# Branch stage of a two-block layer: weight splits ahead of the sigmoid, and the recurrence's first tap and convolution moved within the tile loop

## The reference, cut to what matters

```python
r = sigmoid(einsum('bsnc,ncd->bsnd', xb, w_r) + b_r)      # xb: x in 8 blocks of 128 channels
i = sigmoid(einsum('bsnc,ncd->bsnd', xb, w_i) + b_i)
log_a = (-8.0 * r) * softplus(-a_param)
a = exp(log_a)
u = sqrt(-expm1(2.0 * log_a)) * (i * x)                   # x: causal convolution of 4 taps before it
h_t = a_t * h_(t-1) + u_t                                  # associative_scan over the sequence
y_rnn = h * gelu(gelu_branch)
g = sigmoid(gates.reshape(bsz, s_len, 3, D_MODEL) + gate_b)
m = g[:,:,0] * (y_rnn @ w_br_rnn) + g[:,:,1] * (y_diff @ w_br_diff) + g[:,:,2] * (y_fox @ w_br_fox)
x = x + m @ w_out
```

## Time and profile before

| | before |
|---|---|
| median of 3 runs | 3139.36 us (3138.09 to 3141.09) |
| span of the profiled execution | 3138.1 us |
| PE busy | 2972.4 us, 95% of the span |
| DVE busy | 1407.6 us, 45% |
| ACT busy | 1139.3 us, 36% |
| POOL busy | 734.5 us, 23% |
| attended loop in the trace | about 606 to 869 us |
| recurrence loop in the trace | about 869 to 1077 us |

### The profile page before, as it was taken

How to read it: one execution, slowest core, us unless ns; L and a number is a source line. 1 busy time by engine, 2 the same in 40 slices (tenths; PEclk the granted TensorE clock), 3 DMA queues, 4 the chain that set the end, 5 groups by cost and what they waited for, 6 DMA issues and landing times. The chain is left out here.

```text
span 3138.1 us, 38141 instructions
## 1 busy us (share of the span) xinstructions
PE 2972.4 (95%) x14814; PEld 2394.9 (76%) x14814; DVE 1407.6 (45%) x2138; ACT 1139.3 (36%) x1581; POOL 734.5 (23%) x396
## 2 busy tenths in 40 slices
PE   8997999899999999999999999989899999999988
PEld 6675766588877788877888887867777888878776
DVE  4366044311145413334444344456533556565776
ACT  4354145322156612233222222243442455324543
POOL 2100100022221222212114422111223333123452
PEclk9998999899999999999999999999999999899989
DMA  3110210122211222231111111124333111223343
GB/s 137 43 41 13 62 34 24 23 62 61 67 51 45 64 61 79 103 79 40 47 40 47 60 47 47 40 74 84 65 107 101 48 34 28 108 47 94 131 145 111
DMA packets 250124, 203.63 MB, mean 65 GB/s; under 512 B 38452, under 2 KB 219140, under 8 KB 249996
## 3 DMA queue, kind: packets, MB, share of 16 engines
q1 hardware_dynamic: 247820, 200.84, 22.0%
q10 hardware_dynamic: 2176, 1.05, 0.2%
HBM read 174.69 MB, written 27.16 MB: 64 GB/s over the span
## 5 line engine op out<-in xcount | busy, mean ns | idle before, releaser
L144 POOL TENSOR_TENSOR w_low<-w_raw,w_high 128x1024 fp32r<-128x1024 f32 (+1 forms) x180 | 414.4, 2302 | 1739.7 <-ACT w_high L137 1736.6
L137 ACT ACTIVATE w_high<-w_raw 128x1024 fp32r<-128x1024 f32 (+1 forms) x180 | 179.5, 997 | 293.3 <-PE mix_banks L162 162.3
L162 PE MATMUL ffn_banks<-act_high,w_high 128*128 128x512 f32 x704 | 275.1, 391 | 4.0 <-POOLq L111 4.0
L162 PE MATMUL ffn_banks<-act_low,w_high 128*128 128x512 f32 x704 | 274.9, 390 | 0.0
L162 PE MATMUL ffn_banks<-act_high,w_low 128*128 128x512 f32 x704 | 274.7, 390 | 0.0
L162 PE MATMUL mix_banks<-act_high,w_high 128*128 128x512 f32 x640 | 254.5, 398 | 6.6 <-POOL w_low L144 4.3
L162 PE MATMUL mix_banks<-act_low,w_high 128*128 128x512 f32 x640 | 250.4, 391 | 0.0
L162 PE MATMUL mix_banks<-act_high,w_low 128*128 128x512 f32 x640 | 250.1, 391 | 0.0
L1788 PE MATMUL ffn_banks<-v_high,f_high 128*128 128x512 f32 x352 | 143.4, 407 | 18.2 <-DVE x L1970 9.8
L162 PEld LDWEIGHTS ffn_banks<-act_high,w_high 128*128 128x128 f32 x704 | 132.7, 188 | 32.1 <-POOLq L111 4.4
L1970 DVE TENSOR_TENSOR x<-x,ffn_banks 128x512 f32<-128x512 f32 x176 | 117.1, 685 | 83.7 <-PE ffn_banks L1788 83.7
(11 more groups left out here) (641 smaller groups left out, 6945.8 us busy)
## 6 DMA issues: line engine op xcount, KB each, us to landing
w_raw<-in_w_in SPq DMA_DIRECT2D x106, 512.0 KB, 4.1
w_raw<-in_ffn_up SPq DMA_DIRECT2D x44, 512.0 KB, 3.8
w_raw<-in_w_out SPq DMA_DIRECT2D x24, 512.0 KB, 3.7
v_raw<-in_ffn_down SPq DMA_DIRECT2D x11, 1024.0 KB, 5.0
decay<-acum_rows SPq DMA_DIRECT2D x16, 512.0 KB, 3.6
exp_c<-exp_acum_rows SPq DMA_DIRECT2D x16, 512.0 KB, 5.3
x_ring<-in_x SPq DMA_DIRECT2D x8, 512.0 KB, 10.3
m_part<-gate SPq DMA_DIRECT2D x8, 512.0 KB
```

Source lines behind the costliest of these rows:

```text
L137: act.activation(self.high[slot][:, 0:nk, :], self.raw[slot][:, 0:nk, :], ACT.Copy).then_inc(self.s("high", slot), 1)
L144: pool.tensor_tensor(self.low[slot][:, 0:nk, :], self.raw[slot][:, 0:nk, :], self.high[slot][:, 0:nk, :].bitcast(F32), ALU.subtract).then_ ...
L162: last = pe.matmul(out[:, h, :] if not halves else out[h], w[slot][:, k, :], x[:, k, cols], start=(n == 0), stop=(n == 3 * nk - 1))
```

## The change

In the attended loop the split of slot 0's next turn moves ahead of the sigmoid of the half; the split of slot 1 stays behind it. In the recurrence the first tap becomes a step of its own, `tap3(n)`: tile 0's is made ahead of the loop, and tile n+1's right behind the sqrt of tile n, ahead of the high part of y. It waits for the product of VectorE that reads `xc` (`ix`) in place of `xc_free`, which goes away. On VectorE the convolution becomes `conv(n)`: tile 0's ahead of the loop, tile n+1's between y and y's low part of tile n. VectorE's loop becomes an `over_loop` too. The activations and the VectorE operations are the same in kind and number.

```diff
                 def attended_turn(n, more):
                     for j in two:
+                        turn = n * 2 + j + 1
+                        W.split_high(act, 0, turn if more or j == 0 else RNN_AT)
                         sigmoid_attended(n, j)
-                        turn = n * 2 + j + 1
                         if more or j == 0:
-                            W.split_high(act, 0, turn)
                             W.split_high(act, 1, turn, NK)
                         else:
-                            W.split_high(act, 0, RNN_AT)
                             W.split_high(act, 1, RNN_AT)
...
-                def rnn(n, more):
+                def tap3(n):
                     act.wait_ge(W.s("used", 0), n + RNN_AT + 2)
-                    act.wait_ge(sem("xc_free"), n + 1)
+                    act.wait_ge(sem("ix"), n)
                     act.activation(xc[:, :], flat2(pX), ACT.Identity, scale=taps[:, 3, bass.ds(n, 1)],
                                    bias=bias[:, 0, bass.ds(n, 1)]).then_inc(sem("tap3"), 1)
+
+                def rnn(n, more):
                     if more:
                         W.split_high(act, 0, n + RNN_AT + 1)
...
                     act.activation(Q[:, :], Q[:, :], ACT.Sqrt).then_inc(sem("root"), 1)
-                    if not more:
+                    if more:
+                        tap3(n + 1)
+                    else:
                         last_split(2)
                         last_gate(0)
...
+                act.wait_ge(W.s("used", 0), RNN_AT + 2)
+                act.activation(xc[:, :], flat2(pX), ACT.Identity, scale=taps[:, 3, 0:1], bias=bias[:, 0, 0:1]).then_inc(sem("tap3"), 1)
                 over_loop(act, KD, rnn)
...
-                dve.sem_inc(sem("xc_free"), 1)
...
-                with dve.Fori(0, KD) as n:
+                def conv(n):
                     x = flat2(pX)
                     dve.wait_ge(sem("tap3"), n + 1)
...
                     dve.sem_inc(sem("px_free"), 1)
+
+                def recurrence(n, more):
                     dve.wait_ge(sem("pri_free"), n + 1)
...
-                    dve.tensor_tensor(Q[:, :], Q[:, :], I[:, :], ALU.mult).then_inc(sem("xc_free"), 1)
-                    dve.wait_ge(sem("xc_free"), n + 2)
+                    dve.tensor_tensor(Q[:, :], Q[:, :], I[:, :], ALU.mult).then_inc(sem("u"), 1)
+                    dve.wait_ge(sem("u"), n + 1)
...
                     dve.tensor_tensor(GE[:, :], GE[:, :], Hs[:, :], ALU.mult).then_inc(sem("y"), 1)
+                    if more:
+                        conv(n + 1)
                     dve.wait_ge(sem("yh"), n + 1)
...
+                conv(0)
+                over_loop(dve, KD, recurrence)
```

## The result

The changed kernel takes 3124.15 us (median of 4 runs, 3122.82 to 3124.55) where the kernel before takes 3139.4 us (4 runs). The ratio is 0.995, with a 95% interval of 0.9938 to 0.9961, so 15.2 us less, where 12.0 were forecast. Faster was right: the interval doesn't reach 1.

The account below looks back on a forecast made before the run. TensorE, busy 95% of the span, was taken as the bound, so only its own waits could be won: 5.8 + 6.2 = 12.0 us off the median 3139.36 gives 3127.4 us, range 3125.0 to 3132.0.

Parts of the forecast that it names:

- Both stalls: TensorE's waits: attended gate matmuls for `w_low`, 7 times up to 1.1 us; recurrence block matmuls for the convolution, 6 times 0.9 us.
- The attended term: Attended loop, copy ahead of the sigmoid: 7 x (0.92 - 0.04) = 6.2, less 0.35, gives 5.8 us off.
- the charge of 0.35 us for the table load: Attended loop: load assumed behind the gate product, ahead of the copy, making `w_low` just in time; 0.05 us per half, 7 times.
- T: Attended loop: the moment at which ScalarE sees the gate product finished.
- the 0.04 us of each j=1 half: Attended loop: j=1 to j=0 takes 16.36 us against 16.32 us unstalled; 0.04 us taken off each 0.92 us.
- The recurrence term: Recurrence, tap behind the sqrt and convolution directly behind y: six stalls of 1.04 us go whole, 6.2 us.
- PE's unstalled period, 25.30 us: Recurrence: distance of block matmul starts from tile 6 to tile 7, taken as stall-free, against 26.34 us before.
- The low part beside GpSimd's subtraction: Recurrence, VectorE: y's low part slows from 1.23 us, at most 2.2 us added (pair row 3.42 us), costing 0.
- my ring of 23.1: Recurrence: chain from sigmoid to sigmoid through y, convolution, low part, Gelu and copy, 23.1 us against PE's 25.3 us.
- an estimate of 3136 us: Attended rival: the loop head's load costs more than its length, with a drain, so the stall stays; chance 0.07.
- the rivals: Attended stall stays 0.07; recurrence stall stays, 3133.6 us, 0.06; nothing for PE, 3139.4 us, 0.04; slower, 3147 us, 0.03.
- the slower one: Both loops: PE busy without a gap gets throttled to a clock of 0.96, giving 3147 us; chance 0.03.

Follow-up runs that it names:

- `load_behind`: Changed kernel with ScalarE waiting for the gate product first and alone, so the table load comes behind it; 3125.05 us, ratio 0.9952 (other chip).
- the repeated comparison: Kernel before and changed kernel run again without edits: 3139.27 us (22 runs) and 3125.88 us (5 runs), ratio 0.9959.
- the four kernels on the other chip: Changed kernel with ScalarE's wait or two short activations added, or with convolution or convolution and tap moved back: 3125.05, 3124.55, 3126.59, 3125.96 us; before there 3141.68.
- `tiny_between`: `load_behind` with two one-column activations (sqrt, exp) between the gate product and the copy in each j=0 half; 3124.55 us, ratio 0.9953 (other chip).

## Why the prediction was right and where it failed

The mechanism was right. Both stalls were PE's own, both went whole, no new wait of PE came in the two loops, and their gain moved through to the end. What failed are sizes of terms: of the 3.2 us between 12.0 and 15.2, 1.4 are in the loops and 1.8 outside them.

The attended term was 5.8 us and measured 6.5. The first step that failed is the charge of 0.35 us for the table load: the trace puts the load ahead of T, in idle time, at no cost. The charge was wrong also for the order that I had assumed, as `load_behind` shows with no wait. The second is that I took the 0.04 us of each j=1 half off, 0.3 us in all. All halves take 16.32 us now, and from j=0 to j=0 are 32.64 us instead of 33.60. So a pass lost 0.96 us, with the 0.04 added and not taken off: 7 x 0.96 = 6.7, of which the loop's measure shows 6.5.

The recurrence term was 6.2 us and measured 6.9. I took PE's unstalled period, 25.30 us, from tile 6 to tile 7, but tile 6 is a stalled one, and its start in the earlier trace rows is already late in its own way: behind a stall the first group of block matmuls takes 1.96 us, without one 1.88, and the next product follows that much later. Periods between two unstalled tiles are 25.22 us. The 0.08 us belong to the stall: the seven periods of before are 183.34 us (890.37 to 1073.71), seven of 25.22 are 176.54, and the difference, 6.8, is 1.13 us for each of the six stalls and not 1.04. This is the step that failed in the second term: the unstalled period was mis-sized.

The other 1.8 us of the 15.2 are outside the loops, and none of my terms was for that; the sum put it at nothing, and the range had 1 us for the median. The span less the loops is 2676.5 to 2686.1 us over the ten traces of this study, with either edit, both or none. In the repeated comparison the gain was 13.4 us, the same as the loops' own, and 3125.88 would have been inside the range. So that the first 3124.15 fell below the range is in part chance; with the loops' terms sized right, 13.4 us, the forecast would have been 3126.0. Whether a small part of the outside share belongs to the change isn't settled: the four kernels on the other chip, which all have both stalls gone, came out 15.1 to 17.1 us below their before and gained only 12.6 to 13.4 in the loops, but that before rests on 9 runs that lie 9 us apart.

I had read the clock's lower stretches in the earlier trace rows as a property of the stage; they are partly one of the execution. In one place that made 2.8 us: from the FFN's activation from PSUM (L1879) at 1411.88 to the next of its kind PE needs 39.13 us in the first execution of before (to 1451.01), 36.29 in the second (1413.70 to 1449.99) and 36.29 in the changed kernel (1400.40 to 1436.69). The dip stands in the first alone. What makes the rest of the outside differences isn't shown.

The forecasts of what is late next held. The low part beside GpSimd's subtraction took 2.79 us, inside 1.23 to 3.42. The subtraction runs from 933.00 to 935.39, and the low part ends 1.1 us later, at 936.48. The Trainium skill, "SBUF — State Buffer", section "SBUF: two separate sides", says that a VectorE operation with two SBUF inputs and a GpSimd operation that reads SBUF exclude each other for a whole instruction; the trace agrees. The ring closes: Gelu and the copy behind it end at 940.06, and the sigmoids' turn comes at 940.24, 0.18 us later. That is less than the 2.2 us between my ring of 23.1 and PE's 25.3, because Gelu's table load now stands behind its wait for PE (936.79) where before it was made ahead of it (939.45, with Gelu at 942.17). It looks like the next thing to be late, though 3.1 us of the convolution's slack would hide it at first; no run tried that. In `load_behind` the copy starts 0.01 us behind the load's end. The drain of the Trainium skill, "ScalarE: Activation LUTs", section "What ACT_TABLE_LOAD costs", by which I had an estimate of 3136 us, didn't come. Of the rivals none happened; the clock in the loops stayed at 1.00 through 452 us of unbroken work, which answers the slower one.

## What to carry to other kernels

Look at what ScalarE does between an event of TensorE and the operand that TensorE needs next, table loads included. Here an activation without haste (the sigmoid) and a load that the first activation of a loop body drew could be moved off that path at no cost, and both stalls were gone with a reordering of a few lines. Take a period between two undisturbed neighbours, and never from a disturbed one to an undisturbed one. When a gain of half a per cent is to be forecast, compare two traces of the same kernel first; if their rest differs by as much as a term of the sum, the range has to hold that too.

## What the hardware showed that I had not expected

A wait of PE of the same 3.0 us at the same place was followed by some 7 us at half the clock in one execution of a kernel and by full clock in the next, while other low stretches came in every execution.

A table load doesn't always stand at the same place among the waits of its activation. In the changed kernel the copy waits for the tile and then for T, and the load is made between the two, ahead of T (607.74 for T at 614.30). With a wait for T put first, the load came behind T (615.74). With T as its only wait, the sqrt of `tiny_between` had its load ahead of T (604.95 for T at 613.30). This is no rule yet: Gelu has the same waits in the code of both kernels, and its load stands ahead of the one for PE before and behind it in the changed kernel. Why isn't known.

A weight load of PE that was 0.15 us late cost 0.10 us, 8 times, though the record of the matmul behind it started on time. A late start is better read from the distances of several matmuls than from the first.
